# Constant multiplications for TensorE in five places of a two-block network on one core

## What is computed

```python
def first_block(x, mem, ...):                      # 2 layers: convolution, then attention
    mem_k, mem_v = mem @ w_mem_kv
    for i in range(2):
        y_mix = conformer_conv(x @ conv_w_in) if i == 0 else moba_attention(x @ moba_w_in)
        y_mem = memory_attention(q_mem, mem_k, mem_v)
        x = layer_norm(ALPHA * x + concat(y_mix, y_mem) @ w_o[i], ...)
        f = hierarchical_moe(x, ...)               # 32 experts, 2 chosen for each token
        x = layer_norm(ALPHA * x + f, ...)

def hierarchical_moe(x, ...):
    group = argmax(x @ w_rg + b_rg)                # 4 groups of 8 experts
    top 2 of (x @ w_re + b_re)[group], with softmax weights
    out = sum over experts of weight * (silu(x @ w_gate) * (x @ w_up)) @ w_down

def second_block(x, ...):                          # 2 layers: three attention branches, a merge, an ffn
    for l in range(2):
        h = rmsnorm(x, attn_norm[l]); proj = h @ w_in[l]; ...
    return rmsnorm(x, final_norm)
```

## Time and profile before

| | |
|---|---|
| median of 3 runs | 2197.72 us (2197.64 to 2198.76) |
| profiled execution: span from the first to the last instruction | 2195.8 us |
| what lies around the span, by the median | 1.9 us |
| mean granted clock | 0.985 |
| TensorE matmul busy | 2071.9 us, 94% of the span |
| VectorE busy | 1123.6 us, 51% |
| ScalarE busy | 774.0 us, 35% |
| read from memory | 597.22 MB |

### The profile page before, as it was taken

The page is one execution under the profiler, slowest core; times in us unless marked ns, Lnnn a source line. Parts: engine busy times, 40 slices in busy tenths (PEclk is TensorE's granted clock), DMA queues, the critical chain, the costliest instruction groups (busy, mean ns, idle before and its releaser), DMA issues.

```text
span 2195.8 us, 28571 instructions
## 1 busy us (share of the span) xinstructions
PE 2071.9 (94%) x11872; PEld 1440.3 (66%) x11872; DVE 1123.6 (51%) x1943; ACT 774.0 (35%) x1465; POOL 62.8 (3%) x96
## 2 busy tenths in 40 slices
PE   8989999989979899999899799999999999999998
PEld 7974434334448744343343587998888888998887
DVE  5964332222265632222222667567674676667665
ACT  4751111011034411101010455544554455544552
POOL 3000000000000000000000000010000000010000
PEclk9999999999989999999999899999999999999999
DMA  8628999999982689999999653454554713454552
GB/s 271 219 83 362 428 427 427 427 427 427 425 299 96 269 358 427 428 427 428 427 428 424 233 182 111 154 174 163 184 189 154 258 66 142 173 192 163 192 191 77
DMA packets 132327, 600.20 MB, mean 273 GB/s; under 512 B 6060, under 2 KB 30768, under 8 KB 105824
## 3 DMA queue, kind: packets, MB, share of 16 engines
q1 hardware_dynamic: 127888, 590.37, 67.9%
q10 hardware_dynamic: 3072, 6.74, 0.8%
q0 software_dynamic: 1232, 1.19, 0.4%
HBM read 597.22 MB, written 1.05 MB: 272 GB/s over the span
## 4 chain that ended last, share of the span: by engine, by line
PE 73%; DMA 17%; DVE 6%; ACT 3%; SPq 1%; issue 1%; DVEq 0%; ACTq 0%
PE ps L1717 12%; DMA ring<-in_w_up 10%; PE ps L485 7%; PE ps L1761 7%; PE ps L471 6%; PE ps L473 6%; PE ps L472 6%; DMA rx<-in_w_up 5%; PE ps L484 3%; PE ps L615 2%; PE ps L1010 2%; PE ps L1646 2%; PE ps L1647 1%; PE ps L3146 1%; PE ps L3148 1%; PE ps L3147 1%
## 5 line engine op out<-in xcount | busy, mean ns | idle before, releaser
L447 DVE TENSOR_TENSOR CL<-ring,CH 128x1024 fp32r<-128x1024 f32 x284 | 333.3, 1214 | 201.9 <-ACT CH L442 200.4
L1717 PE MATMUL ps<-ring,ARM 128*64 128x512 f32 x1024 | 349.1, 602 | 26.1 <-DMA ring<-in_w_up 20.2
L1717 PE MATMUL ps<-rx,ARM 128*64 128x512 f32 x1024 | 349.8, 602 | 24.5 <-DMA rx<-in_w_up 16.5
L442 ACT ACTIVATE CH<-ring 128x1024 fp32r<-128x1024 f32 x284 | 283.5, 1046 | 125.1 <-PE ps L3148 57.3
L1735 DVE TENSOR_TENSOR ARM<-ARM,ps 128x512 f32<-128x512 f32 x32 | 22.0, 687 | 438.7 <-PE ps L1717 438.7
L485 PE MATMUL ps<-XTHL,CH 128*128 128x512 f32 x704 | 240.6, 396 | 0.0
L1717 PEld LDWEIGHTS ps<-rx,ARM 128*64 128x64 f32 x1024 | 111.3, 139 | 183.0 <-issue 143.6
L1717 PEld LDWEIGHTS ps<-ring,ARM 128*64 128x64 f32 x1024 | 112.0, 139 | 175.7 <-issue 135.3
L471 PE MATMUL ps<-XTHL,CH 128*128 128x256 f32 x752 | 219.5, 292 | 0.5 <-ACT AB L1536 0.5
L473 PE MATMUL ps<-XTHL,CL 128*128 128x256 f32 x752 | 212.7, 283 | 0.0
L472 PE MATMUL ps<-XTHL,CH 128*128 128x256 f32 x752 | 212.6, 283 | 0.0
(11 more groups left out here) (456 smaller groups left out, 3757.5 us busy)
## 6 DMA issues: line engine op xcount, KB each, us to landing
rx<-in_w_gate SPq DMA_DIRECT2D x34, 2048.0 KB, 24.4
ring<-in_w_up SPq DMA_DIRECT2D x32, 2048.0 KB, 27.1
ring<-in_w_gate SPq DMA_DIRECT2D x30, 2048.0 KB, 25.4
ring<-in_w_down SPq DMA_DIRECT2D x30, 2048.0 KB, 26.6
ring<-in_w_ffn SPq DMA_DIRECT2D x30, 2048.0 KB, 8.2
rx<-in_w_up SPq DMA_DIRECT2D x28, 2048.0 KB, 27.2
rx<-in_w_down SPq DMA_DIRECT2D x26, 2048.0 KB, 27.1
ring<-in_w_in SPq DMA_DIRECT2D x14, 2048.0 KB, 9.0
```

Source lines behind the costliest of these rows:

```text
L442: a.e.activation(pc.hi[:, cs], pc.ap[:, cs], ACT.Copy).then_inc(act_done, a.put("hi", pc.k, q))
L447: v.e.tensor_tensor(pc.lo[:, cs], pc.ap[:, cs], pc.hi[:, cs].bitcast(F), ALU.subtract).then_inc(dve_done, v.put("lo", pc.k, q))
L1717: i = p.e.matmul(b[64 * x:64 * x + 64, :], m.XG[:, c, s0 + 64 * x:s0 + 64 * x + 64], us[x].ap[:, c, :], start=c == 0, stop=c == 7)
```

## The change

A helper `p_busy(n, x, bank)` multiplies a 128 x 128 part of a constant by a 128 x 256 part of it, n times, into a bank whose earlier content has been read. Nobody reads the results, and nothing counts them. It is called in five kinds of places: five times ahead of the memory's transposes, with ones that VectorE writes to `GB` first; six times ahead of the first weights' matmuls; eight times in each routing, behind the logits' transposes; behind the experts, 14 times in layer 0 and 23 times in layer 1; and four times between the two halves of the transposes that follow layer 0's experts. ScalarE waits for the convolution's last first-stage matmul, `u 11`, before it lets `GB` be loaded; the same engine waited for that matmul before, a few instructions earlier.

```diff
+        def p_busy(n, x, bank=None):
+            i = spun[0] % 8 + 1 if bank is None else bank
+            i %= 8
+            last = held.get(i)
+            if last is not None:
+                if a.has(*last):
+                    p.wait_ge(act_done, a.at(*last))
+                if v.has(*last):
+                    p.wait_ge(dve_done, v.at(*last))
+            for _ in range(n):
+                p.e.matmul(banks[i][:, 0:256], x[:, 0:128], x[:, 0:256], start=True, stop=True)
...
-        def p_transposed(tag, src, ready):
+        def p_transposed(tag, src, ready, between=None):
             for t in range(2):
+                if t and between:
+                    between()
...
+            idle = GB.rearrange("p g d -> p (g d)")
+            p.wait_ge(dve_done, v.at("idle"))
+            p_busy(5, idle)
             p_transposed("mem", MEM, mem_ready)
             pc = p_piece("mix0", 0)
+            p_busy(6, CST)
...
         def dve_memory():
+            v.e.memset(GB[:, 0, 0:256], 1.0).then_inc(dve_done, v.put("idle"))
...
+            a.wait_ge(pe_done, p.at("u", 11))
             load_gb(I["ln1_g"][0], I["ln1_b"][0])
...
-            p_transposed("x1", X, x_ready)
+            p_transposed("x1", X, x_ready, lambda: p_busy(4, CST))
...
             i.then_inc(pe_done, p.put("router sums", l))
+            p_busy(8, CST)
             b = take(("places", l))
...
             pe_over(l, some)
+            p_busy((14, 23)[l], CST, B_X)
             p.name("end", "moe", l)
```

## The result

The changed kernel takes 2208.22 us (median of 5 runs, 2205.75 to 2212.64) against 2198.68 us for the kernel before beside it (5 runs, 2197.64 to 2199.26): a ratio of 1.0049, 95% interval 1.0038 to 1.0060. It is slower by some 10 us where 6 us less were forecast. The profiled execution took 2208.39 us, with a span of 2206.5 us and a mean granted clock of 0.989 (0.985 before). The mean clock rose, and the kernel got slower all the same.

What follows compares the result with a forecast made beforehand. TensorE bounds the kernel (73% of the chain) by its own work, its waits and its clock. Terms 1.7 + 2.3 + 2.1 + 0.2 - 0.5 = 5.8 us take 2197.7 to 2191.9 us, range 2189.8 to 2194.8.

Steps and rivals of the forecast that it cites:

- Does it fit?: All filler places: each filler ends before TensorE's next work, 0.4 to 1.2 us ahead; branch priced at VectorE's 0.55 us.
- if the instructions behind the branch come so late that the clock falls first: Rival, behind both layers' experts: filler runs at 0.87 us each and overruns, 10 us slower, 2208 us; chance 0.05.
- The routings: Gathers of both layers: warm clock shortens the cold work, gaining 1.7 us in layer 0 and 2.3 in layer 1.
- The filler leaves only 0.4 us and 0.2 us wholly idle: Routings: argument against a lost bridge, since 1.83 us idle was enough for the clock to fall at 52 us.
- one bridge does not hold: Rival, routings or between the layers: clock falls behind thin work, up to 2.1 us lost, 2194.0 us; chance 0.20.
- the pause of the transfers: Experts' transfers stand still from 174 to 179 us, so an earlier gather moves them earlier; both routings count in full, 4.0 us.
- Between layer 0's experts and layer 1: Second transposes to scores: 24 of 56 matmuls run cold; warm, VectorE limits the gain, taken as 2.1 us.
- The rival's doubt about transposes: Between the layers, within the 0.20 rival: if transposes do not hold the clock, up to 2.1 us are lost.
- Beginning of the second block: `p_folded` behind layer 1's experts: 0.35 us at most from the clock, gain taken as 0.2 us.
- The start: Before the convolution: no gain, as weights land at 36.2 us anyway; a longer gap loses 0.5 us.
- some 3.2 us: Start: TensorE's idle gap before it starts again at 52.51 us grows from 1.83 us to this.
- A rule weighed: Start: the skill's 3 us gap rule would make the loss 1.7 us, 2193.1 us; the sum kept the trace's row.

Runs made afterwards that it cites:

- experiment 6: The changed kernel with none of the loops left in TensorE's code inside the branch of `pe_over`, only three waits behind it: 2194.62 us, ratio 0.9985.
- Experiment 3: The changed kernel with the 14 and 23 multiplications moved ahead of the branch of `pe_over`, all else as changed: 2195.14 us, ratio 0.9986.

## Why the prediction was wrong

**"Does it fit?" is the step that failed.** It took the branch's cost from VectorE's chain, 0.55 us, and let the filler start at 627.0 and 1227.4. TensorE's branch costs 5.57 and 5.78 us. Under VectorE's branch there was either less code to skip or it had been fetched, which was not tested; the row of another engine could not price this one. The row that spoke of TensorE, the wait of 7.3 us for VectorE, only bounded the delay from above: anything up to 7.3 us could have lain under it. I named the rival ("if the instructions behind the branch come so late that the clock falls first"), worked out 2208 us for it, and gave it 0.05. The working was good in total (2208.2 measured), but by luck: it put 9.5 and 4.9 us of overrun where a net 7.5 and 3.1 were lost, and took off 4.0 us from the routings, which did not come. It left the delay itself out and let the whole filler run cold, while the delay is 5.6 and 5.8 us and only the first third of the 14 ran cold. What was wrong is the chance. A delay bounded by 0 and 7.3 us, with a threshold of 2.7 us, asked for more than that.

**"The routings": the mechanism was right, the bridge was too short.** "The filler leaves only 0.4 us and 0.2 us wholly idle" took the 0.19 us ahead of the gather from an execution in which the place matmuls ran cold. Warm, they end earlier, and 0.92 us are idle. So the rival "one bridge does not hold" was true of both routings here: in the changed kernel it takes 6.70 and 7.40 us from the gathers to the first weights (168.25 to 174.95, 770.92 to 778.32), where it took 6.93 and 7.51. With two further multiplications the gain is 1.7 us in layer 0 (forecast 1.7) and 1.6 in layer 1 (forecast 2.3: the term shortened the whole cold stretch, but its first 1.7 us, from 764.96 to 766.65 us in the warm run, are set by VectorE's next positions and do not shrink; 0.43 x 1.7 = 0.7 us too much), and the experts pass it on, as argued from the pause of the transfers.

**"Between layer 0's experts and layer 1": right, once the filler stands ahead of the branch.** 12.96 us became 11.07: 1.9 us, forecast 2.1. The rival's doubt about transposes came true in the one trace without the four multiplications, and did not in the five that have them.

**"Beginning of the second block": 0.2 forecast, 0.0 found** (7.88 and 7.89 us). **"The start": a loss of 0.5 forecast, none found** (1.0001), though runs that tell 2 us can't test 0.5; the gap of "some 3.2 us" came out at 3.2.

**A rule weighed.** The Trainium skill (TensorE: Matmul & The Clock Gate, "Why this matters for your kernels") warns of gaps of more than about 3 us; in the run without the four the clock fell within a gap of 2.10 us, and in the trace of before behind 1.83 us, while 3.15 us left it up in experiment 6. So the runs do not agree with the figure: a shorter gap is no safety, and one of that length is not always a loss.

The measured terms, 1.7, 1.6 and 1.9, add up to 5.2 us; the version that has all three is 5.3 us faster. That agreement is partly luck, since all three are taken against one execution, the trace of before, and the cold stretches differ between executions. In the traces without filler at these places they took 6.63 to 6.93 us (gather of layer 0, three traces), 6.63 to 7.51 (layer 1, three) and 11.85 to 13.24 (transposes to scores, four). Against their means the terms are 1.5, 1.1 and 1.4, together 4.0 us; the measured 3.1 to 7.5 us hold both sums. The forecast of 5.8 us was near the mark for a kernel with the filler ahead of the branch, two multiplications more in each routing and none at the start, not for this one.

## What to carry to other kernels

An idle stretch that is put down to one wait may hide a second delay beneath it; whoever fills it with work that doesn't wait meets the second one, so ask what else could keep the engine from starting there. Filler goes ahead of a branch that skips much code, never behind it, and must end even if it starts cold (14 multiplications took 6.2 us in the one place and 8.0 us, partly cold, in the other). A bridge is as good as its thinnest part, and that part has to be measured in the warm kernel: four and two small multiplications decided over some 2 and 3 us in the traces, while the 23 decided over nothing. And one trace isn't enough to size a clock effect: take several executions of both kernels.

## What was unexpected of the hardware

- A taken branch on TensorE over two rounds of loop code delayed the next matmul by 5.4 to 5.8 us, over one round by 4.05 and 3.14 us, over three waits by nothing. The matmul resumed 2.5 to 2.7 us behind the start of the 16 KB packet in all of them. What shrank with half of the code was the time from the last matmul to the packet, 1.8 us in layer 0 in place of 3.2 to 3.6; why stays open.
- An idle time of 3.15 us left the clock at 1.00 in one execution, while with 0.92 us behind a few thin matmuls it fell within 10 of 14 gathers. A gap's length alone did not decide it.
- The clock also falls while TensorE is fully busy, for a few us, at places that differ between executions. Experiment 3 has one (stretch, columns as in the earlier trace rows):

```profile
131.00:135.00 4.00, 4.00 (x23) 4.00 (x22) 3.65 (x8) 1.50 (x4) 0.00 (x0) 0.57 0.00 0
```

  Nothing in the profile announces it. The traces of both kernels have several such stretches; they are likely part of the spread of single runs, which was not tested.
- More clock was not less time: the slowest kernel of the study has a mean of 0.989, and the one with ten multiplications in the routings alone, 2193.42 us, has 0.985.
